# Cache pages of a paged attention step: three groups of four slots used in turn

## What is computed

```python
def fox_sample(q, k, v, log_f, k_past, v_past, lf_past):      # 8 samples, 2048 past rows each
    s = einsum(q, concat(k_past, k)) * HEAD_DIM ** -0.5 + decay + mask
    return softmax(s) @ concat(v_past, v)

# token mixer, for prompt and samples
z = rms_norm(h) @ w_in
merged = sigmoid(g_a) * (rwkv_branch(z) @ proj_a) + sigmoid(g_b) * (fox_branch(z) @ proj_b)
h += merged @ w_out
# then 32 experts, 4 groups, top 2 inside the best group
h += sum_e combine[e] * ((silu(x @ w1[e]) * (x @ w3[e])) @ w2[e])
```

## Time and profile before

| | us |
|---|---|
| median of 3 unprofiled runs | 904.72 (903.98 to 906.97) |
| profiled execution, its own time | 901.19 |
| its span, first to last instruction | 899.6 |
| TensorE busy | 767.6 (85% of the span) |
| VectorE, ScalarE, GpSimd busy | 374.3, 186.5, 149.6 |
| bytes moved by DMA | 220.27 MB, mean 245 GB/s over the span |

### The profile page before, as it was taken

How to read it: one execution, slowest core, us unless ns; L and a number is a source line. 1 busy time by engine, 2 the same in 40 slices (tenths; PEclk the granted TensorE clock), 3 DMA queues, 4 the chain that set the end, 5 groups by cost and what they waited for, 6 DMA issues and landing times. The chain is left out here.

```text
span 899.6 us, 20892 instructions
## 1 busy us (share of the span) xinstructions
PE 767.6 (85%) x8753; PEld 461.3 (51%) x8753; DVE 374.3 (42%) x683; ACT 186.5 (21%) x424; POOL 149.6 (17%) x300
## 2 busy tenths in 40 slices
PE   3999899998878979967887697989869997899985
PEld 2445566665566656743454565545744444444421
DVE  3022532338942235466872775724262222422213
ACT  3001222216331111012421322222111110111112
POOL 8400030007040020022043343333000000000000
PEclk9999899998978969968899799999969998999998
DMA  8533141122320212428899999987929999999993
GB/s 321 199 129 144 49 146 58 47 97 63 109 77 20 74 47 51 100 90 298 294 377 415 421 349 420 415 334 281 379 113 382 423 424 423 424 417 424 421 426 114
DMA packets 53239, 220.27 MB, mean 245 GB/s; under 512 B 21871, under 2 KB 24218, under 8 KB 28826
## 3 DMA queue, kind: packets, MB, share of 16 engines
q1 hardware_dynamic: 45456, 184.66, 53.2%
q0 software_dynamic: 7040, 34.10, 9.7%
q10 hardware_dynamic: 650, 0.18, 0.1%
HBM read 211.82 MB, written 7.09 MB: 243 GB/s over the span
## 5 line engine op out<-in xcount | busy, mean ns | idle before, releaser
L230 PE MATMUL bank<-arena 128*128 128x320 f32 x256 | 83.2, 468 | 3.5 <-PEq L112 3.5
L208 POOL DMA_DIRECT2D arena<-in_cv x112 | 59.2, 528 | 129.2 <-PE bank L1860 100.0
L530 PE MATMUL bank<-arena 128*128 128x336 f32 x224 | 70.9, 472 | 4.2 <-DVE arena L687 4.2
L2549 DVE TENSOR_TENSOR arena<-arena,bank 128x512 f32<-128x512 f32 x40 | 27.5, 687 | 106.9 <-PE bank L2337 103.8
L1497 DVE STREAM_TRANSPOSE arena<-arena 128x2048 f32<-128x2048 f32 x28 | 63.1, 2288 | 11.8 <-DMA arena<-in_ck 10.6
L2360 PE MATMUL bank<-arena 128*32 128x512 f32 x512 | 62.9, 596 | 2.7 <-DMA arena<-in_w_exp 2.0
L504 PE MATMUL bank<-arena 128*128 128x512 f32 (+1 forms) x144 | 62.3, 593 | 0.0
L230 PEld LDWEIGHTS bank<-arena 128*128 128x128 f32 x256 | 48.8, 201 | 24.7 <-issue 8.5
L530 PEld LDWEIGHTS bank<-arena 128*128 128x128 f32 x224 | 43.8, 200 | 27.2 <-issue 9.7
L1860 PE MATMUL bank<-arena 128*16 128x128 f32 x1024 | 36.2, 306 | 21.8 <-issue 19.1
L1315 ACT ACTIVATE arena<-bank 128x384 f32<-128x384 f32 (+6 forms) x63 | 26.0, 444 | 123.0 <-PE bank L230 46.2
(11 more groups left out here) (476 smaller groups left out, 1104.0 us busy)
## 6 DMA issues: line engine op xcount, KB each, us to landing
arena<-in_w_exp SPq DMA_DIRECT2D x99, 1024.0 KB, 20.0
arena<-in_ck SPq DMA_DIRECT2D x120, 256.0 KB, 7.0
arena<-in_cv POOLq DMA_DIRECT2D x112, 256.0 KB, 6.8
arena<-in_w_gate SPq DMA_DIRECT2D x8, 1024.0 KB, 4.8
arena<-in_w_za SPq DMA_DIRECT2D x7, 1024.0 KB, 6.8
arena<-in_w_zb SPq DMA_DIRECT2D x6, 1024.0 KB, 14.2
arena<-in_cv SPq DMA_DIRECT2D x16, 256.0 KB, 3.7
arena<-in_w_proj SPq DMA_DIRECT2D x8, 512.0 KB, 11.4
```

Of the source, the lines that this page charges most:

```text
L208: eng.dma_start(tile[n:P:4, :], src[bass.ds(page, 1)].rearrange("a (p j) n -> (a p) (j n)", j=4))\
L230: mm = nc.tensor.matmul(bank[b][:, 0:TM], w[:, k, a, :], xnT[:, k, NMETA:T], start=(k == 0), stop=(k == KT - 1))
L530: mm = nc.tensor.matmul(bank[j % 2][:, 0:T], w[:, k, (j % 2) * P:(j % 2 + 1) * P], xnT[:, k, :], start=(k == 0), stop=(k == KT - 1))
```

## The change

Keys and values now share three groups of four slots: group 0 is slots 0 to 3, group 1 is 11 to 14, group 2 is 4 to 7. Keys of sample b go into group `KEYS_IN[b]`, its values into `VALUES_IN[b]`. For b from 1 on both are the same group: once scores(b) are done the values of b are loaded over its keys. Keys of sample b (3 and later) go where the values of sample b - 3 have been weighed, quarter by quarter. `proj_load(sp, 1, 0)` moves ahead of `key_loads(3)`. The expert tiles loaded ahead, and two tiles of `w_out`, follow the slots as they come free, and `ORDER` changes with them. Values have two sets of semaphores in place of one. No arithmetic is added or removed.

```diff
@@ -148,7 +148,7 @@
         place = slot + [arena[:, base + i * SLOT:base + (i + 1) * SLOT] for i in range(3)]
         place += [arena[:, odd_at + i * SLOT:odd_at + (i + 1) * SLOT] for i in range(4)]
         place += [arena[:, w_at + i * SLOT:w_at + (i + 1) * SLOT] for i in range(3)]
-        ORDER = [2, 3, 11, 12, 13, 14, 4, 5, 6, 7, 9, 15, 17, 8, 0, 1, 16, 10]
+        ORDER = [2, 3, 4, 5, 6, 7, 11, 12, 13, 14, 9, 15, 17, 8, 0, 1, 16, 10]
         FIRST = len(ORDER)
         assert 3 * SLOT <= ATILES * ZC + NPAIR * T
 
@@ -1488,9 +1488,18 @@
         stage_p = [pre(TM) for _ in range(2)]
 
         NPOST = NGT - GT_PAIRS
-        key_slot = lambda b, m: m if b % 2 == 0 else 11 + m
-        kneed = lambda b, m: first_fill[m] + 64 * (b // 2 + 1) if b % 2 == 0 else 64 * (b // 2 + (m < 2))
-        keys = [arena[:, at:at + 4 * SLOT].rearrange("p (x j k) -> p x j k", j=2 * NH, k=32) for at in (0, odd_at)]
+        KEYS_IN, VALUES_IN = (0, 1, 0, 2, 1, 0, 2, 1), (2, 1, 0, 2, 1, 0, 2, 1)
+        key_slot = lambda b, m: (m, 11 + m, 4 + m)[KEYS_IN[b]]
+        value_slot = lambda b, m: (m, 11 + m, 4 + m)[VALUES_IN[b]]
+
+        def kneed(b, m):
+
+            group = KEYS_IN[b]
+            loads = 64 * KEYS_IN[:b + 1].count(group)
+            return loads + (first_fill[m], -64 * (m >= 2), first_fill[4 + m] + 64)[group]
+
+        keys = [arena[:, at:at + 4 * SLOT].rearrange("p (x j k) -> p x j k", j=2 * NH, k=32)
+                for at in (0, odd_at, 4 * SLOT)]
 
         def turn_into(b, m):
             tile = place[key_slot(b, m)]
@@ -1624,8 +1633,8 @@
 
         valid = ident.rearrange("p (g c) -> p g c", g=NPAIR)[:, :, 0:2 * DS]
 
-        vpool = [S(f"v_full{m}") for m in range(4)]
-        vneed = lambda b, m: (vpool[m], 64 * b) if b else (full[4 + m], first_fill[4 + m] + 64)
+        vpool = [[S(f"v_full{i}_{m}") for m in range(4)] for i in range(2)]
+        vneed = lambda b, m: (vpool[b % 2][m], 64 * ((b + 1) // 2)) if b else (full[4 + m], first_fill[4 + m] + 64)
 
         def page_part(s, n):
             return s[:, n * BW:(n + 1) * BW]
@@ -1691,16 +1700,16 @@
 
         def out_fill(c):
 
-            return full[out_slot[c]], (48, 16, kneed(6, 0) + 16, kneed(6, 1) + 16)[c]
+            return full[out_slot[c]], (48, 16, kneed(5, 0) + 16, kneed(5, 1) + 16)[c]
 
         def place_fills(s):
 
             if s < 2:
-                return kneed(6, s) + 16
+                return kneed(5, s) + 16
             if s < 4:
-                return kneed(6, s)
+                return kneed(5, s)
             if s < SLOTS:
-                return first_fill[s] + 64
+                return kneed(6, s - 4)
             return {8: 0, 9: 0, 10: 16, 15: 64, 16: 48, 17: 32}[s] if s not in range(11, 15) else kneed(7, s - 11)
 
         def ahead(sp, s):
@@ -1716,7 +1725,7 @@
                     for m in range(4):
                         pages = [sp.value_load(pt_row[0:1, b * NPAGES + 4 * m + n:b * NPAGES + 4 * m + n + 1])
                                  for n in range(4)]
-                        sp.wait_ge(S("sco_ps"), b - 1)
+                        sp.wait_ge(*((S("sco_ps"), 1) if b == 2 else (S("pv_ps"), 4 * (b - 3) + m + 1)))
                         s = key_slot(b, m)
                         for n in range(4):
                             page_load(sp, place[s], n, A["ck"], pages[n], full[s])
@@ -1728,9 +1737,9 @@
                 gates_load(0)
                 proj_load(sp, 0, 1)
                 key_loads(2)
-                key_loads(3)
                 sp.wait_ge(S("kept_rw"), 16 * NPAIR * (DB + 1))
                 proj_load(sp, 1, 0)
+                key_loads(3)
                 sp.wait_ge(S("fill_ps"), 4)
                 proj_load(sp, 1, 1)
                 for i in range(NT - 1):
@@ -1744,13 +1753,11 @@
                 out_load(sp, 0)
                 out_load(sp, 1)
                 key_loads(7)
-                sp.wait_ge(S("sco_ps"), DB - 1)
-                out_load(sp, 2)
-                out_load(sp, 3)
+                for n, c in enumerate((2, 3)):
+                    sp.wait_ge(S("pv_ps"), 4 * 5 + n + 1)
+                    out_load(sp, c)
                 for s in (2, 3):
-                    ahead(sp, s)
-                sp.wait_ge(S("sco_ps"), DB)
-                for s in (11, 12, 13, 14):
+                    sp.wait_ge(S("pv_ps"), 4 * 5 + s + 1)
                     ahead(sp, s)
                 sp.wait_ge(S("scn_ps"), DB)
                 for r, c in ((UP, slice(0, HALF)), (DN, slice(HALF, DM))):
@@ -1759,8 +1766,11 @@
                 sp.dma_start(lnb2, ln_row[1, :].partition_broadcast(P)).then_inc(S("ln2_in"), 16)
                 sp.dma_start(wr, A["w_r"]).then_inc(S("wr_in"), 16)
                 for m in range(4):
+                    sp.wait_ge(S("pv_ps"), 4 * (DB - 2) + m + 1)
+                    ahead(sp, 4 + m)
+                for m in range(4):
                     sp.wait_ge(S("pv_ps"), 4 * (DB - 1) + m + 1)
-                    ahead(sp, 4 + m)
+                    ahead(sp, 11 + m)
                 sp.wait_ge(S("oT_ps"), DB)
                 ahead(sp, 9)
                 sp.wait_ge(S("sb_ps"), 1)
@@ -1783,9 +1793,9 @@
                     for m in range(4):
                         pages = [pool.value_load(pt_row[0:1, b * NPAGES + 4 * m + n:b * NPAGES + 4 * m + n + 1])
                                  for n in range(4)]
-                        pool.wait_ge(S("pv_ps"), 4 * (b - 1) + m + 1)
+                        pool.wait_ge(S("sco_ps"), b + 1)
                         for n in range(4):
-                            page_load(nc.gpsimd, slot[4 + m], n, A["cv"], pages[n], vpool[m])
+                            page_load(nc.gpsimd, place[value_slot(b, m)], n, A["cv"], pages[n], vpool[b % 2][m])
                 pool.wait_ge(S("m_ready"), ND)
                 pool.wait_ge(S("sco_ps"), DB)
                 nc.gpsimd.tensor_copy(gs_keep, gates[:, :, SEQ:TM]).then_inc(S("gs_kept"), 1)
@@ -1820,7 +1830,7 @@
                             for i in range(4):
                                 r = slice(32 * i, 32 * i + 32)
                                 mm = nc.tensor.matmul(bank[i][32 * g:32 * g + 2 * DS, :], qs[r, b, j, :],
-                                                      keys[b % 2][r, :, j, :], start=False, stop=(t == 3))
+                                                      keys[KEYS_IN[b]][r, :, j, :], start=False, stop=(t == 3))
                     mm.then_inc(S("sco_ps"), 1)
                     if b == 0:
                         pe.wait_ge(S("o_zero"), 1)
@@ -1859,7 +1869,7 @@
                         for g in range(NPAIR):
                             mm = nc.tensor.matmul(bank[7][32 * g:32 * g + 2 * DS, 0:P],
                                                   pT[:, n, 2 * DS * g:2 * DS * (g + 1)],
-                                                  page_part(slot[4 + m], n % 4)[:, g * P:(g + 1) * P],
+                                                  page_part(place[value_slot(b, m)], n % 4)[:, g * P:(g + 1) * P],
                                                   start=(n == 0), stop=False)
                         if n % 4 == 3:
                             mm.then_inc(S("pv_ps"), 1)
```

## The result

Over 20 runs of each kernel the median went from 905.66 us to 910.51 us; the ratio is 1.007 with a 95% interval of 1.0051 to 1.0089, or 6.3 us (4.6 to 8.1). The forecast was +2.4 us, and 907.1 us; 910.5 lies inside the stated range. The direction was right, but the forecast loss was less than half of the measured one.

A forecast was written before the change was run, and what follows sets the result against it. "moe" was taken to last as long as its bytes, passing on gains or losses of "cache" one for one. 4.2 + 1.5 - 2.5 - 0.8 = +2.4 us on the 904.7 median gave 907.1 us, range 897.5 to 911.5.

The forecast's parts named there:

- Values 1 earlier: At 444 to 456 us, values 1 and the moved projection load fill the DMA hole: 3.4 us won.
- the 390 GB/s that were to show it: Sign that the hole is filled: DMA at over 390 GB/s from 445 to 456 us in the changed kernel.
- Keys 3 later: Before scores(3), keys 3 wait some 4 us longer; at most 1.5 us on VectorE, covered, so priced at nothing.
- Values 3 and the gates: Before scores(4), values 3 go out from 488 us and delay the second gates 5.0 us: plus 4.2 us.
- Rival A: Gates before scores(4) are not delayed, scores(4) come 2.5 us sooner: 898.9 us in all, chance 0.25.
- Clock: TensorE idles twice around weigh(2) and scores(4) and runs at half clock: plus 1.5 us (0 to 2).
- From sample 4 on: Later samples of "cache": values arrive on time and the 0.95 us wait goes: minus 2.5 us (0 to -4).
- rival B: Keys become late at every sample, some 2.5 us at each of samples 5 and 6: 912.1 us, chance 0.15.
- the two signs that the prediction had named for being wrong: Second sigmoid on ScalarE starts by 504 us, or VectorE waits for keys 5, 6 or 7.
- End of "cache": TensorE's 2.46 us stop at 604.78 us may shrink: minus 0.8 us (0 to -3).

The follow-up runs named there:

- e2: Changed kernel, but the first load of the second projection weights stands behind keys 3 again; ratio to the kernel before 1.0104 (1.0064 to 1.0143).
- e3: Changed kernel, but the values of sample 3 wait until the second gates have landed; ratio to the kernel before 1.001 (0.9985 to 1.0035).
- e13: Changed kernel, but values 3 wait for the second gates and values 7 for the weighing of sample 6; ratio to the kernel before 0.9967 (0.9938 to 0.9996).
- e5: Changed kernel run again unchanged, for a second profile; ratio to the kernel before 1.0093 (1.0052 to 1.0134).
- e1: Changed kernel, but each quarter of values also waits for the weighing of the sample before; ratio to the kernel before 1.0014 (0.9982 to 1.0046).
- e11: Changed kernel, but the last sample's values wait for the weighing of the sample before; ratio to the kernel before 1.0029 (0.9995 to 1.0063).
- e7: Kernel before, with 2.1 MB not needed yet (second projection weights' second half, prompt rows) sent behind the second gates; ratio 1.0005 (0.9974 to 1.0035).
- e9: Kernel before, with the first load of the second projection weights moved ahead of keys 3; ratio 1.001 (0.998 to 1.0039).
- e14: Kernel before, first load of second projection weights ahead of keys 3, two output weight loads ahead of keys 6, second run; ratio 0.999 (0.9956 to 1.0023).
- e10: Kernel before, first load of second projection weights ahead of keys 3, two output weight loads ahead of keys 6, first run; ratio 0.9982 (0.9958 to 1.0006).
- e4: Kernel before run again unchanged, for a second profile; ratio 1.0003 (0.9976 to 1.0029), medians 903.83 against 904.38 us.
- e8: Kernel before, but the four expert tiles sent at scores(7) wait until sample 6 is weighed; ratio 1.0101 (1.0049 to 1.0152).

## Why the prediction was right and wrong, step by step

*Values 1 earlier: half the size, and by the other part.* The hole filled to 341 GB/s from 282; (341 - 282) / 415 of 12 us are 1.7 us, half of the 3.4 forecast, and far from the 390 GB/s that were to show it. In e2, where values 1 go out early but the weights do not, it is 287: what filled it was the moved weights.

*Keys 3 later, priced at nothing: right in the sum.* VectorE waited more than I allowed (2.62 us, not 1.5), TensorE's clock fell before weigh(1) and scores(3) came 3.4 us late. But the cover held: in e3 and e13 scores(3) are just as late (63.8) and scores(4) earlier than before.

*Values 3 and the gates: right in mechanism, too large.* Forecast 5.0 us, measured 2.7 and 3.4 (82.3 to 85.0 and 85.8 in the table). Scores(3) were late, so values 3 went out at 490.6 and not at 488. That the sum came this near is partly luck. Set against e3, whose gates land at 80.6, values 3 cost 4.4 and 5.2 us, where the forecast had 8.4 (5.0 and the 3.4 in hand), and the hole gave 1.7 and not 3.4: both were half the size and nearly cancelled. e3 confirms the cause: it holds only these values and gains 5.4 us at scores(4). Rival A, in which the gates are not delayed, had scores(4) 2.5 us sooner than before (its sum gives 511.75 and not 511.5, so 2.3); in e3 and e13, where values 3 are held, they are 2.1 and 1.7 us sooner.

*Clock, plus 1.5: about right, at another place.* The last 8 fill matmuls ran at the lower clock, 3.21 us (e5: 3.68) where 24 took 5.45 before, so 1.4 and 1.9 us more than 1.8; in the first profile 0.4 us came on top at the start of scores(4). The 128 score matmuls behind, for which the term had been priced, ran at full clock, 4.58 us. Together with the step above the forecast for scores(4) was plus 5.7, and measured were plus 3.3 and 4.6. Scores(4) to scores(5) took 21.9 and 21.3 us, before 21.4.

*From sample 4 on, minus 2.5: wrong.* Scores(4) to scores(7): 73.5 and 75.6 us against 74.4 and 74.1 before, so between minus 0.9 and plus 1.5. The wait for values 4 went, and a wait for the second quarter of keys 6 came (the row at 544.37), 2.27 us in one profile and 4.13 in the other: that is rival B in small, and one of the two signs that the prediction had named for being wrong. By itself it is not the loss: e1 and e3 have this wait too (2.84 and 2.65 us), and their runs are at 1.0014 and 1.001. What the step overlooked is the hole at 512 to 524 us. Values had gone out early, keys 6 were not yet allowed, and neither queue had anything to send.

*End of "cache", minus 0.8: the step that failed.* It said that the stop inside weigh(6) "may shrink". It grew, from 2.46 and 2.54 us to 3.84 and 3.55, by 1.0 to 1.4 us, and in all six profiles with early values 7 it is 3.29 us or more. I had counted how many tiles are loaded there and not what runs at the same moment: values 7, which used to start with weigh(6), now go out at 596.3 us, ahead of it, with six small loads and four tiles right behind. e11 undoes this alone and gets 1.0029 for 1.007; e13 adds it to e3 and gets 0.9967 for 1.001. By the runs early values 7 so cost 3.7 and 3.9 us, each with an uncertainty of nearly its own size. Against minus 0.8 that is a difference of some 4.5 us, and with the step before (1.6 to 4.0 us above its forecast) more than the whole miss of 3.9; the steps ahead of scores(4) came out 1.1 to 2.4 us below theirs.

In the two profiles of the changed kernel scores(7) to weigh(7) took 4.0 us more than before, and 2.3 to 2.5 of these are the 16 fill matmuls at the lower clock (9.43 and 9.62 us for 7.13). These 2.3 us can't be put down to the change: in e7, e9 and e14, whose block ends as in the kernel before, the clock falls there too (8.55 to 9.97 us). Why it falls is not settled: it fell behind stops of 1.35 us (e11), 2.47 (e9) and 3.84, and stayed full behind 1.10 (e13), 2.46 (before) and 3.29 (e3), so it does not go by the length of the stop alone. That early values 7 lengthen the stop is shown; how the 3.7 and 3.9 us of the runs divide between stop and clock is open.

## What to carry to other kernels

When buffers are made to come free earlier, ask of each load that now starts sooner what else is queued at that moment, and who needs that first: values 3 sent beside the gates cost some 5 us there, and held back they ran at 420 GB/s in a stretch that was else at 235. Where the DMA engines are full, a new order of the same bytes may only move a wait (e7). That filling a hole is worth its bytes is not shown: e10 and e14 filled one, and their 0.2 and 0.1% are not clear of noise. Compare places of profiles with several executions beside them: two of one kernel that agree within 0.3 us (before, e4) did not bound the scatter. And a wait that holds back one group of loads (e3, e13) can be worth more than the freedom that a new layout of buffers gives.

## What the runs showed of the hardware

TensorE stops in the middle of a loop of matmuls that has no wait in it, behind the second of eight, in all 15 profiles in which the DMA engines are busy there. The profiler lists one packet of 16 KB on an instruction queue at that moment; TensorE goes on after it. The DMA queues of the kernel before from 602 to 604 us, where TensorE starts again at 604.78:

```profile
q8 instruction: 1, 0.02, 3.0%
```

The changed kernel from 605 to 607 us (TensorE again at 607.94), e11 from 604 to 607 (608.17) and e13 from 600 to 602 (602.67):

```profile
q8 instruction: 1, 0.02, 3.1%
```

```profile
q8 instruction: 1, 0.02, 3.5%
```

```profile
q8 instruction: 1, 0.02, 3.6%
```

From the end of the packet, which takes 1.0 to 1.7 us, to the next matmul it is 1.2 to 1.3 us in all four. The packet itself starts 4.3 us after weigh(6) in the kernel before, 5.7 in the changed one, 2.4 and 2.9 in e11 and e13, and 1.1 in e8, where the engines are idle and there is no stop. From this I read that TensorE's instructions travel through the same DMA engines as data and come late when these are full; the profile does not say whose instructions the packet holds. The Trainium skill ("Runtime: NRT & Kernel Launch", Instruction fetch mechanics) says that each sequencer fetches its instructions by a DMA queue of its own in blocks of 16 KiB, which the packets here agree with, and that this is hidden behind the issue of instructions, which, if the reading is right, 1.1 to 3.9 us of stop inside weigh(6) contradict.
